# Gate chunks first, and turned queries and keys by VectorE and DMAs, in a two-block layer stack on one core

## What is computed

```python
h = rmsnorm(x, mix_norm[l])
hq, hf, hi, hg, aq, ak, av, ga, gb = split(h @ w_in[l])      # 1024 x 10752 weights
f = lb + (1 - lb) * sigmoid(hf)                              # recurrence: 8 heads of 128
q_a, k_a, v_a, log_f = silu(hq), 1 - f, hi, log(f)
o_a = hgrn2_chunk_scan(q_a, k_a, v_a, log_f)
y_a = (rms(o_a) * hgrn_out_norm[l] * silu(hg)) @ w_branch_a[l]
q_b = apply_rope(rms(heads(aq)) * qn, cos, sin)              # 3 groups x 4 heads x 128
k_b = apply_rope(rms(heads(ak)) * kn, cos, sin)
for g, (window, dilation) in enumerate(((128, 1), (512, 4), (2048, 16))):
    o_g, lse_g = dilated_window_attention(q_b[g], k_b[g], v_b[g], window, dilation)
y_b = (softmax over groups of lse, weighted sum of o_g) @ w_branch_b[l]
x = x + (sigmoid(ga) * y_a + sigmoid(gb) * y_b) @ w_out[l]
```

## Time and profile before

| | |
|---|---|
| Time, median of 3 runs | 2658.0 us (2656.32 to 2658.15) |
| The profiled execution | 2656.8 us, its span 2655.0 us |
| TensorE busy | 2645.1 us (100% of the span) |
| VectorE busy | 1967.1 us (74%) |
| ScalarE busy | 1427.8 us (54%) |
| GpSimd busy | 166.1 us (6%) |
| DMA | 489.26 MB, mean 184 GB/s |
| Granted TensorE clock | 0.9 or more of full speed in all 40 slices |

### The profile page before, as it was taken

How to read it: one execution, slowest core, us unless ns; L and a number is a source line. 1 busy time by engine, 2 the same in 40 slices (tenths; PEclk the granted TensorE clock), 3 DMA queues, 4 the chain that set the end, 5 groups by cost and what they waited for, 6 DMA issues and landing times.

```text
span 2655.0 us, 42138 instructions
## 1 busy us (share of the span) xinstructions
PE 2645.1 (100%) x15660; PEld 2240.7 (84%) x15660; DVE 1967.1 (74%) x2660; ACT 1427.8 (54%) x2021; POOL 166.1 (6%) x98
## 2 busy tenths in 40 slices
PE   9999999999999999999999999999999999999999
PEld 8888888888888888888888888888888888888888
DVE  6777767777777876777776888567777769876676
ACT  5446565445446565544545767554454466765543
POOL 0000000000000000000000132000000012210000
PEclk9999999999999999999999999999999999999999
DMA  7556455655555545556555754546555665454553
GB/s 239 190 175 207 150 169 169 202 190 195 193 193 196 166 160 183 176 190 196 180 190 190 230 167 165 185 149 205 190 178 192 212 199 185 162 188 159 186 190 130
DMA packets 324380, 489.26 MB, mean 184 GB/s; under 512 B 17312, under 2 KB 204064, under 8 KB 324256
## 3 DMA queue, kind: packets, MB, share of 16 engines
q1 hardware_dynamic: 323968, 487.47, 56.0%
q10 hardware_dynamic: 288, 0.07, 0.0%
HBM read 478.02 MB, written 1.05 MB: 180 GB/s over the span
## 4 chain that ended last, share of the span: by engine, by line
PE 94%; DVE 2%; ACT 2%; issue 1%; DMA 0%; POOL 0%; SPq 0%; ACTq 0%; DVEq 0%
PE bank L371 48%; PE bank L573 22%; PE bank L571 12%; PE bank L476 5%; PE bank L941 2%; PE bank L984 1%; PE bank L390 1%; DVE w_low L333 1%; ACT w_high L328 0%; PE bank L976 0%; DVE log_decay L2040 0%; PE bank L1647 0%; POOL decay L2118 0%; PE bank L1167 0%; ACT log_decay L1802 0%
## 5 line engine op out<-in xcount | busy, mean ns | idle before, releaser
L333 DVE TENSOR_TENSOR w_low<-raw,w_high 128x2048 fp32r<-128x2048 f32 x435 | 1008.3, 2319 | 397.5 <-ACT w_high L328 397.1
L328 ACT ACTIVATE w_high<-raw 128x2048 fp32r<-128x2048 f32 x435 | 831.1, 1912 | 474.5 <-PE bank L571 243.0
L371 PE MATMUL bank<-w_high,xT_parts 128*128 128x512 f32 x2304 | 739.4, 395 | 0.0
L573 PE MATMUL bank<-xT_parts,w_high 128*128 128x512 f32 x2560 | 618.6, 391 | 0.0
L573 PEld LDWEIGHTS bank<-xT_parts,w_high 128*128 128x128 f32 x2560 | 472.1, 188 | 92.2
L371 PEld LDWEIGHTS bank<-w_high,xT_parts 128*128 128x128 f32 x2304 | 432.6, 188 | 89.9
L371 PE MATMUL bank<-w_low,xT_parts 128*128 128x512 f32 x1152 | 448.7, 389 | 0.0
L571 PEld LDWEIGHTS bank<-xT_parts,w_low 128*128 128x128 f32 x2560 | 334.5, 191 | 16.7
L571 PE MATMUL bank<-xT_parts,w_low 128*128 128x256 f32 x2560 | 339.4, 282 | 0.0
L668 ACT ACTIVATE siluT<-gateT 128x256 f32<-128x256 f32 x160 | 66.8, 417 | 407.3 <-DVE gateT L724 406.9
L371 PEld LDWEIGHTS bank<-w_low,xT_parts 128*128 128x128 f32 x1152 | 216.6, 188 | 42.6
(11 more groups left out here) (308 smaller groups left out, 2684.7 us busy)
## 6 DMA issues: line engine op xcount, KB each, us to landing
raw<-in_w_in SPq DMA_DIRECT2D x288, 512.0 KB, 4.6
raw<-in_ffn_w_in SPq DMA_DIRECT2D x176, 512.0 KB, 4.5
raw<-in_ffn_wd SPq DMA_DIRECT2D x88, 512.0 KB, 4.1
raw<-in_ffn_w_out SPq DMA_DIRECT2D x88, 512.0 KB, 4.1
raw<-in_ffn_wg SPq DMA_DIRECT2D x86, 512.0 KB, 3.8
raw<-in_ffn_wu SPq DMA_DIRECT2D x86, 512.0 KB, 4.7
raw<-in_w_out SPq DMA_DIRECT2D x32, 512.0 KB, 4.2
raw<-in_w_branch_a SPq DMA_DIRECT2D x16, 512.0 KB, 5.3
```

Source lines behind the costliest of these rows:

```text
L328: nc.scalar.activation(wh[slot][:], raw[slot][:], ACT.Copy).then_inc(high_done[slot], 1)
L333: nc.vector.tensor_tensor(wl[slot][:], raw[slot][:], wh[slot][:].bitcast(F32), ALU.subtract).then_inc(low_done[slot], 1)
L371: mm = pe.matmul(o[:, 0:n], x[:, rows], w[slot][:, col + j * n:col + (j + 1) * n], start=start and first, stop=stop and last)
L573: mm = pe.matmul(bank[:], wh[s][:, w], xhl[:, kt, :, :], start=kt == 0, stop=False, skip_group_check=True)
```

## The change

- The chunk order becomes HF, HF+512, HQ, HQ+512: both gate chunks first. Each of the four chunks gets its own landing tile (`hland`), so the DMAs home no longer wait for a reader. Key scaling moves from VectorE's steps 6 and 11 to 5 and 7, the scans from 6 and 13 to 7 and 8; both Ln groups stand in ScalarE's step 7 (were 6 and 12), the query copies in 8 and 10 (were 4 and 8).
- Attention queries and keys are no longer transposed by TensorE. VectorE rotates in three full-width operations and transposes 32x32 blocks (`rotated2`), after its weight split, except for the last section. The gains are multiplied into cosine and sine tables by GpSimd, two products a section. SP issues four DMAs per section ahead of unit 30, 32, 34, 36, 38 and 39. ScalarE drains five sections by four copies each, in steps 27 to 35.
- The keys of the first group come last and aren't drained: the heads read them from the landing tile `akT0`.
- The scale of keys is one instruction instead of eight. The gate product of the recurrence's output is split over steps 29 and 31, and its transposes use four PSUM banks.

```diff
-CHUNKS2 = [HQ, HF, HQ + 512, HF + 512, HI, HI + 512, HG, HG + 512, AV, AV + 512,
-           AQ, AQ + 512, AQ + 1024, AK, AK + 512, AK + 1024, AV + 1024, GA, GA + 512, GB, GB + 512]
+CHUNKS2 = [HF, HF + 512, HQ, HQ + 512, HI, HI + 512, HG, HG + 512, AV, AV + 512,
+           AQ, AQ + 512, AQ + 1024, AK + 512, AK + 1024, AK, AV + 1024, GA, GA + 512, GB, GB + 512]
...
@@ mix2_sp @@
-                    if c == 2:
-                        sp.wait_ge(hq_out, at2(lay, 2, 1))
-                    if c == 3:
-                        sp.wait_ge(k_done, at2(lay, 2, 1))
-                        sp.wait_ge(lnf_done, at2(lay, 2, 1))
-                    squares_home(sp, hsq[c % 2], hland[c % 2], hT_in[c % 2])
+                    squares_home(sp, hsq[c % 2], hland[c], hT_in[c])
...
+                a, odd = divmod(u - AQ0 - (7 if u == AQ0 + 17 else 8), 2)
+                if odd == 0 and 0 <= a < (6 if u == AQ0 + 17 else 5):
+                    sp.wait_ge(asq_turned, at2(lay, 6, a + 1))
+                    if 1 < a < 5:
+                        sp.wait_ge(sec_out2, at2(lay, 5, a - 1))
+                    squares_home(sp, asq, aland[a], aT_in[a % 2])
...
@@ mix2_tail (TensorE) @@
-            a, odd = divmod(u - AQ0 - 3, 2)
-            if odd == 0 and 0 <= a < 6:
...
-                for i in range(2):
-                    tr = turn_tokens(pe, wk[2 + i], stg[a % 2], 2 * i)
-                tr.then_inc(sec_T2, 1)
...
                 if hd == 0:
-                    pe.wait_ge(sec_out2, at2(lay, 6, 6))
-                    pe.wait_ge(oaTl_done, at2(lay, 8, 8))
+                    pe.wait_ge(sec_out2, at2(lay, 5, 5))
+                    pe.wait_ge(aT_in[1], at2(lay, 192, 192))
+                    pe.wait_ge(oaTl_done, at2(lay, 8, 4))
...
@@ mix2_act @@
-                for hf, step in ((0, 4), (1, 8)):
+                for hf, step in ((0, 8), (1, 10)):
...
-                for hf, step in ((0, 6), (1, 12)):
+                for hf, step in ((0, 7), (1, 7)):
...
+                a, odd = divmod(u - AQ0 - 5, 2)
+                if odd == 0 and 0 <= a < 5:
+                    act.wait_ge(aT_in[a % 2], at2(lay, 192, 64 * (a // 2 + 1)))
...
+                    for c in range(4):
+                        r = nc.scalar.activation(dst[:, :, c], aland[a][:].rearrange("p k h t (i c) -> p (h t) k i c", c=4)[:, :, :, :, c], ACT.Copy)
                     r.then_inc(sec_out2, 1)
...
@@ VectorE @@
+        def rotated2(dve, lay, a):
+
+            x, xr, xs = [y[:].rearrange("p t (h s e) -> p t h s e", h=ATT_HEADS, s=2) for y in (stg[a % 2], rtm, rsq)]
+            cos, sin = [tabs[a][:, n].rearrange("p t (s e) -> p t s e", s=2).unsqueeze(2).broadcast_to((P, TT, ATT_HEADS, 2, DH // 2)) for n in range(2)]
+            dve.wait_ge(tab_done, at2(lay, 6, a + 1))
+            nc.vector.tensor_tensor(xr, x[:, :, :, ::-1, :], sin, ALU.mult)
+            if a > 0:
+                dve.wait_ge(aT_in[(a - 1) % 2], at2(lay, 192, 64 * ((a + 1) // 2)))
+            link(dve, nc.vector.tensor_tensor(xs, x, cos, ALU.mult))
+            link(dve, nc.vector.tensor_tensor(stg[a % 2][:], rsq[:], rtm[:], ALU.add))
+            squares_turned(stg[a % 2], asq).then_inc(asq_turned, 1)
...
+                if u == AQ0 + 12:
+                    rotated2(dve, lay, 5)
...
                     split_low(dve, 2, slot_of(u + 2), lay, mix_use(u + 2))
+                a, odd = divmod(u - AQ0 - 2, 2)
+                if odd == 0 and 0 <= a < 5:
+                    rotated2(dve, lay, a)
...
-                for hf, step, scan in ((0, 6, 6), (1, 11, 13)):
+                for hf, step, scan in ((0, 5, 7), (1, 7, 8)):
...
-                if odd == 1 and 0 <= a < 6:
+                if odd == 1 and ATT_GROUPS <= a < 6:
...
+                    r = nc.vector.tensor_tensor(x8, x8, rsa[:, a, :].unsqueeze(2).broadcast_to((P, 8, DH)), ALU.mult)
...
@@ mix2_pool @@
+                    tab = tabs[a][:].rearrange("p n t (s e) -> p n t s e", s=2)
+                    nc.gpsimd.tensor_tensor(tab[:, 0], cos, gain.unsqueeze(1).broadcast_to(each), ALU.mult)
+                    nc.gpsimd.tensor_tensor(tab[:, 1], sin, gain[:, ::-1, :].unsqueeze(1).broadcast_to(each), ALU.mult).then_inc(tab_done, 1)
```

More of the change, by code:

```diff
@@ L244, in build @@
         hsq = [over(f"hg_squares{i}", [P, 1024], 74 + 4 * i) for i in range(2)]
-        hland = [over(f"hg_turned{i}", [P, 4, 4, TT, 32], 82 + 4 * i) for i in range(2)]
+        hland = [over(f"hg_turned{c}", [P, 4, 4, TT, 32], kib) for c, kib in enumerate((82, 86, 90, 66))]
         hgt = over("hg_gate", [P, TT, D], 46)
@@ L251, in build @@
         av = over("a_v", [P, 3, TT, 512], 82)
-        akT = over("akT", [P, 12, SEQ], 0)
+        akT0 = over("akT0", [P, 4, 4, TT, 32], 0)
+        akT = over("akT", [P, 8, SEQ], 4)
+        asq = over("a_squares", [P, 1024], 74)
+        tabs = [over(f"rope_tables{a}", [P, 2, TT, DH], kib) for a, kib in enumerate((72, 28, 72, 28, 30, 28))]
+        aland = [over(f"a_turned{a}", [P, 4, 4, TT, 32], kib) for a, kib in enumerate((12, 16, 12, 16, 20))] + [akT0]
         ob = over("o_b", [P, TT, 512], 12)
@@ L1693, in mix2_tail @@
                     pe.wait_ge(oh_out, at2(lay, 2, 2))
[L1694 to L1695 removed]
                 for i in range(2):
[L1697 removed]
+                    turn_tokens(pe, wk[2 * i0 + i], hgt, 4 * i0 + 2 * i).then_inc(oaT_done, 1)
             hd, odd = divmod(u - ATT0 - 1, 2)
@@ L1732, in mix2_tail @@
                 if hd < ATT_HEADS:
-                    q, k = aqT[:, hd, :], akT[:, hd, :]
-                    pe.matmul(wk[0][:, 0:P], q[:, 0:P], k[:, 0:P], start=True, stop=True)
+                    q, k = aqT[:, hd, :], akT0[:, :, hd, :, :].rearrange("p a t i -> p t a i")
+                    pe.matmul(wk[0][:, 0:P], q[:, 0:P], k[:, 0], start=True, stop=True)
                     pe.matmul(wk[0][:, P:384], q[:, P:SEQ], k, start=True, stop=True).then_inc(dsc_done, 1)
@@ L2053, in mix2_dve @@
                     nc.vector.tensor_scalar(msa[:], ssa[:], times / DH, times * EPS, ALU.mult, ALU.add).then_inc(ams_done, 1)
-                if u == HG0 + NHG + 4:
-                    dve.wait_ge(oh_out, at2(lay, 2, 2))
-                    dve.wait_ge(hgs_done, at2(lay, 1, 1))
-                    for hf in range(2):
+                for hf in range(2):
+                    if u == HG0 + NHG + 4 + 2 * hf:
+                        dve.wait_ge(oh_out, at2(lay, 2, 2))
+                        dve.wait_ge(hgs_done, at2(lay, 1, 1))
                         g = hgt[:, :, halves(hf)]
@@ L2062, in mix2_dve @@
                 a, odd = divmod(u - AQ0, 2)
[L2063 removed]
+                if odd == 1 and ATT_GROUPS <= a < 6:
                     x8 = stg[a % 2][:].rearrange("p t (h d) -> p (t h) d", d=DH)
[L2065 to L2072 removed]
+                    dve.wait_ge(apow_done, at2(lay, 6, a + 1))
+                    r = nc.vector.tensor_tensor(x8, x8, rsa[:, a, :].unsqueeze(2).broadcast_to((P, 8, DH)), ALU.mult)
                     link(dve, r)
@@ L2127, in mix2_pool @@
                     nc.gpsimd.tensor_tensor(rsa[:, a, :], msa[:], neghalf[:, 0:8], ALU.pow).then_inc(apow_done, 1)
+                    if a == 0:
+                        pool.wait_ge(kblk_in, at(lay, 16, 16))
+                    elif a == 1:
+                        pool.wait_ge(A_done, at2(lay, NHG, NHG))
+                    else:
+                        pool.wait_ge(asq_turned, at2(lay, 6, a - 1))
+                    cos, sin = [kblk[:, k:k + TT * DH].rearrange("p (t s e) -> p t s e", t=TT, s=2) for k in (K2_COS, K2_SIN)]
+                    gain = cols[:, C2_QK + WEIGHT_OF[a] * DH:C2_QK + (WEIGHT_OF[a] + 1) * DH].rearrange("p (s e) -> p s e", s=2)
+                    each = (P, TT, 2, DH // 2)
+                    tab = tabs[a][:].rearrange("p n t (s e) -> p n t s e", s=2)
+                    nc.gpsimd.tensor_tensor(tab[:, 0], cos, gain.unsqueeze(1).broadcast_to(each), ALU.mult)
+                    nc.gpsimd.tensor_tensor(tab[:, 1], sin, gain[:, ::-1, :].unsqueeze(1).broadcast_to(each), ALU.mult).then_inc(tab_done, 1)
         t_mix = {1: dict(sp=mix1_sp, pe=mix1_pe, act=mix1_act, dve=mix1_dve, pool=mix1_pool),
```

76 lines of the change are left out of this document (21 added, 55 removed).

## The result

| | before | after |
|---|---|---|
| Time, median of 11 runs each, taken together | 2657.4 us | 2664.3 us (2663.4 to 2666.6) |
| Ratio after to before | | 1.0025, 95% interval 1.0017 to 1.0032 |
| Span of the profiled execution | 2655.0 us | 2662.3 us |
| TensorE busy | 2645.1 us | 2638.1 us |
| VectorE busy | 1967.1 us | 1966.4 us |

The changed kernel is 6.9 us slower. The forecast was 2660 with a range of 2647 to 2667: the range holds the result, the likeliest case's own range (2653 to 2663) ends 1.3 us short of it, and at 0.25% (interval 0.17 to 0.32%) it lies just outside the 0.2% that I called no change.

The account below looks back on a forecast made before the run. TensorE was taken as the bound (94% of the chain), VectorE as nearly a second. Per layer 3.4 us lost in the recurrence less 2.1 gained in the key stretch, twice +2.6 in all, gave 2660 us, range 2647 to 2667.

Parts of the forecast that it names:

- the likeliest case: The forecast itself: recurrence loses 3.4 us a layer, query and key stretch gains 2.1; 2653 to 2663, chance 0.49.
- VectorE not fitting in the key stretch: Rival: a table product takes over some 0.7 us of VectorE, using up the gain; 2665 to 2667, chance 0.17.
- the clock: Rival: TensorE's clock falls to 1.2 GHz after level 0's 2.8 us wait, 5.5 us a layer; 2671, chance 0.04.
- The walk to level 0: Recurrence, ScalarE and VectorE queues: level 0's products done at 1504.5 instead of 1500.93, so TensorE waits 2.8 us.
- The key stretch: Query and key stretch up to unit 36: transposes save 5.2 us a layer, TensorE stalls 3.2; 2.1 gained.
- GpSimd's tables: Table products in the key stretch: 0.4 us of VectorE's time each, 2.0 in the window, range 0 to 4.
- the added DMAs on SP: Four per section, 24 a layer, 0.61 us each on SP; 2.4 us ahead of a weight load, expected to hide.
- the last section's landing: Last keys' DMAs need 4.9 to 9.3 us against 7.7 available: zero wait at the median, 1.6 at worst.
- Half way: Rival: recurrence costs 0.3 to 0.8 us, key stretch gives 4.0; about 7 faster, 2651, chance 0.18.
- TensorE stays the only bound: Rival: level 0 isn't late and the recurrence's stall goes too; 13.6 us faster, 2644, chance 0.12.

Follow-up runs that it names:

- gates_only: Kernel before with only the recurrence's part of the change: gate chunks first and their steps moved, TensorE's transposes of queries and keys kept; 2662.4 us.
- no_tables: Changed kernel without GpSimd's table products: VectorE rotates with plain cosines and sines, gains left out of queries and keys; 2654.7 us.
- warm_filler: Changed kernel with 28 small matmuls put on TensorE ahead of its wait for unit 36's low part, in both layers; 2660.4 us.
- late_rotation: Changed kernel with the last section's rotation and transpose moved behind unit 36's low part on VectorE; 2661.4 us.
- all_four_separate: Changed kernel with first Ln and scan earlier, GpSimd's subtraction before VectorE's low part, tables early and each announced separately, last rotation behind unit 36's low part; 2646.2 us.
- early_tables: Changed kernel with three key sections' table products moved from steps 28, 30 and 32 to step 25, right behind the recurrence; 2658.3 us.
- before_gpsimd_first: Kernel before with one wait added: in the recurrence VectorE starts its low part only after GpSimd's subtraction for the next level; 2660.2 us.

## Why the prediction was right, and where it fell short

**The direction and the two mechanisms were right.** Slower, because level 0 comes late and because VectorE isn't ready at unit 36. Forecast +2.6, measured +6.9. That the range holds the result is partly luck: its part above 2663 was there for a case that didn't come, VectorE not fitting in the key stretch, and the clock that filled it had its own forecast at 2671.

**The walk to level 0** gave 1504.5. VectorE's timeline of after:

```profile
1503.74 0.42 DVE L1928 TENSOR_TENSOR decayed<-decay,hkT 128x256 f32<-128x256 f32 x1
...
1516.51 0.43 DVE L1928 TENSOR_TENSOR decayed<-decay,hkT 128x256 f32<-128x256 f32 x1
...
1540.93 0.41 DVE L1928 TENSOR_TENSOR decayed<-decay,hkT 128x256 f32<-128x256 f32 x1
```

Level 0's are done at 1504.16. (On the way the walk has the first Ln group done at 1490.3, where its own terms add up to 1490.1; the scan behind it started at 1490.2.) From level 0 to level 2 I had 12.9 us and the trace has 12.8; from level 2 to level 6 24.65 against 24.4. Level 6 ends at 1541.34 (forecast 1542.05). The cost, +3.4 a layer in the forecast, was +2.9 to +3.0: the three small deviations all have one sign. gates_only, with this part alone, has +2.8 and +2.7.

**The key stretch.** I had the last transposition end at 1663.6 on the clock of before. In after it ends at 1666.98 with the recurrence 2.85 us behind, so 1664.1. TensorE wanted unit 36 at 1662.7 by the forecast; it had done unit 35 at 1665.25 less 2.85, 1662.4. The wait was 3.2 by the forecast and 4.0 in the trace. GpSimd's tables, the one cost with no row before, I put at 0.4 each and 2.0 in the stretch; no_tables measured 0.43 and 2.6. Without the half clock the stretch gave 4.6 less 3.3, 1.3 a layer, where I had 2.1 (my own terms, 5.2 less 3.2, make 2.0).

**The step that failed is the clock.** Without its fall at unit 36 warm_filler stands at +3.1 us in all, against my +2.6. That this is so near is luck in part: the recurrence cost 0.5 less a layer than forecast, the stretch gave 0.8 less. The other 3.8 us of the measured 6.9 are half clock behind the wait at unit 36. I had the mechanism among the rivals, at 0.04, and asked for it at the wrong place: at level 0's wait of 2.8 us, while my own sum had a longer one, 3.2 us, at unit 36. My reason against it was a gap of 1.94 us in rows 4 with the clock kept at 1.00, which says nothing about 4 us. Its price, a whole unit at half clock, 5.5 us, was too high as well: 1.6 and 2.2 us were lost per fall.

**What was priced right at nothing:** TensorE waited for no landing in after, the added DMAs on SP hid, and the last section's landing was covered as long as its rotation stood ahead of unit 36's low part. The landing itself took 2.6 us per DMA here, not the 5.0 of the median in rows 9. late_rotation shows how little slack there was even so: 2.9 us of waiting once the rotation stood behind.

**The rivals.** Half way needed GpSimd's products to fall in gaps, and they mostly don't. The slower case by VectorE asked for more than 0.7 us per table; it was 0.43. TensorE stays the only bound came close to true only in all_four_separate, with its further edits. The one that came true besides the forecast was the clock.

## What to carry to other kernels

Work taken off TensorE is worth only what the engine that feeds it can follow: before a change of this kind, walk the feeder's queue to the first unit behind the stretch, and where it ends late, mend that queue in the same change. A wait of TensorE can have a second price, the granted clock behind it: here it fell at each of the 14 profiled waits of 2.8 us and more, and at most of those of 2.3 to 2.4, unless something race-free ran in the wait. Put that price into the sum, at the longest wait that the sum itself has. Where GpSimd and VectorE meet, ask which is on the chain and let that one start first, and give each small product its own signal.

## What the runs showed of the hardware

**The granted clock falls behind waits far shorter than a unit.** In the profiled executions of all kernels here: at each of the 14 waits of 2.8 to 4.2 us at unit 36 or at the scores it fell to 0.50; at the two of 2.3 us at unit 36 (early_tables) too; at level 0's 2.4 us (gap 2.6) it fell in 9 of 14 cases, not always in the same layer of like kernels; at 1.9 us and less never, the end of the program aside, where TensorE runs out of work. The runs without a trace say that the lower end is a matter of chance: the mean clocks of early_tables have room for no fall at all in four runs, and those of before_gpsimd_first, whose longest wait in this mixer is 1.9 us, show lost clock in eight of eleven. It stayed at 0.50 for 3.4 us, or for 6.8, and each of the five that stayed for 6.8 began before the wait was over. With the same wait of 4.0 us S was 4.8 to 5.0 in the first case and 5.6 to 6.1 in the second, so two executions of the same kernel can differ by about 1 us a layer from this alone. The eleven runs of the changed kernel have mean clocks from 0.996 to 0.999.

The Trainium skill (TensorE: Matmul & The Clock Gate, HAM oscillation — how this bites in real kernels) says that in a thin matmul kernel, which waits for DMAs between its tiles, TensorE is throttled again in each wait and every tile starts at the lower clock. The waits of this case agree with the mechanism; the shortest wait here behind which a trace shows it is 2.3 us.

**A power on GpSimd is dear when blocked.** 128x8 elements take 1.64 us alone and 3.61 us when VectorE's low part has started first, 2.0 us more (GpSimd's timeline of after):

```profile
1605.61 1.64 POOL L2117 TENSOR_TENSOR rstd_a<-ms_a,neghalf 128x8 f32<-128x8 f32 x1 [11.97 <-DVE ms_a L2049]
...
1656.25 3.61 POOL L2117 TENSOR_TENSOR rstd_a<-ms_a,neghalf 128x8 f32<-128x8 f32 x1 [7.09 <-DVE ms_a L2049]
```
